# Four RMS norms whose scale is applied late: sums by one product with ones and roots over 512 columns, in place of eight narrow products and a spread

## The reference, cut to what matters

```python
def rms_norm(x, g):
    y = xf * lax.rsqrt(jnp.mean(xf * xf, axis=-1, keepdims=True) + EPS)
    return (y * g.astype(jnp.float32)).astype(x.dtype)

for i in range(DEPTH):                      # DEPTH = 2
    u = rms_norm(h, norm_mix_g[i])
    ...
    h = h + merged @ w_o[i]
    m = rms_norm(h, norm_mlp_g[i])
    h = h + jnp.square(jax.nn.relu(m @ w_up[i])) @ w_down[i]
    e = rms_norm(h, norm_ple_g[i])
    h = h + jax.nn.sigmoid(e @ w_ple_gate[i]) * (p[i] @ w_ple_proj[i])
```

## Time and profile before

| | us |
|---|---|
| median of 3 runs | 3181.43 (3177.78 to 3186.06) |
| the profiled execution, its own time | 3182.89 |
| its span | 3181.1 |
| TensorE busy | 3137.8 (99%), granted clock 0.993 on the mean |
| VectorE busy | 1957.7 (62%) |
| ScalarE busy | 1225.0 (39%) |
| GpSimd busy | 674.5 (21%) |
| mean DMA rate | 108 GB/s |

### The profile page before, as it was taken

How to read it: one execution, slowest core, us unless ns; L and a number is a source line. 1 busy time by engine, 2 the same in 40 slices (tenths; PEclk the granted TensorE clock), 3 DMA queues, 4 the chain that set the end, 5 groups by cost and what they waited for, 6 DMA issues and landing times.

```text
span 3181.1 us, 36265 instructions
## 1 busy us (share of the span) xinstructions
PE 3137.8 (99%) x14870; PEld 2547.1 (80%) x14870; DVE 1957.7 (62%) x2630; ACT 1225.0 (39%) x1645; POOL 674.5 (21%) x499
## 2 busy tenths in 40 slices
PE   9999999999999999999999999999999999999998
PEld 7877888888887788888888766778888888888887
DVE  7555657566666566677756556656555589963433
ACT  4234442233432344422244345643334353442222
POOL 1000000000100010699971133302433001110001
PEclk9999999999999999999999999999999999999999
DMA  3222233454222223355432100023333322222221
GB/s 132 77 95 84 87 139 141 164 197 180 91 88 90 80 86 111 132 202 186 172 113 100 31 25 28 18 84 129 118 124 115 144 86 101 103 95 95 95 104 67
DMA packets 55622, 342.41 MB, mean 108 GB/s; under 512 B 5984, under 2 KB 7840, under 8 KB 18208
## 3 DMA queue, kind: packets, MB, share of 16 engines
q1 hardware_dynamic: 54080, 337.46, 29.6%
q10 hardware_dynamic: 1376, 2.62, 0.2%
HBM read 327.47 MB, written 12.58 MB: 107 GB/s over the span
## 4 chain that ended last, share of the span: by engine, by line
PE 84%; DVE 9%; ACT 4%; issue 2%; POOL 1%; DMA 0%; DVEq 0%; ACTq 0%; SPq 0%; POOLq 0%
PE PS L264 83%; DVE wl L273 2%; DVE UL L273 1%; DVE FA L281 1%; ACT PB L270 1%; PE PS L267 1%; DVE SC L273 1%; ACT SC L270 1%; ACT UH L270 1%; DVE PB L273 1%; DVE SC L281 1%; POOL PB L277 1%; DVE ST L293 1%; DVE PS L273 0%; ACT wh L270 0%
## 5 line engine op out<-in xcount | busy, mean ns | idle before, releaser
L264 PE MATMUL PS<-UH,wh 128*128 128x512 f32 (+1 forms) x2120 | 836.3, 394 | 4.3 <-DVE UL L273 1.8
L264 PE MATMUL PS<-UH,wl 128*128 128x512 f32 (+1 forms) x2120 | 823.0, 388 | 0.0
L264 PE MATMUL PS<-UL,wh 128*128 128x512 f32 (+1 forms) x2120 | 822.9, 388 | 0.0
L273 DVE TENSOR_TENSOR wl<-raw,wh 128x2048 fp32r<-128x2048 f32 (+2 forms) x255 | 563.4, 2211 | 386.1 <-ACT wh L270 386.0
L264 PE MATMUL PS<-RH,wh 128*128 128x512 f32 (+2 forms) x1640 | 645.5, 394 | 2.1 <-ACT FA L270 1.1
L264 PE MATMUL PS<-RH,wl 128*128 128x512 f32 (+2 forms) x1640 | 639.0, 390 | 0.0
L264 PE MATMUL PS<-RL,wh 128*128 128x512 f32 (+2 forms) x1640 | 638.9, 390 | 0.0
L270 ACT ACTIVATE wh<-raw 128x2048 fp32r<-128x2048 f32 (+2 forms) x255 | 452.4, 1780 | 242.4 <-DMA raw<-in_wall 170.4
L264 PEld LDWEIGHTS PS<-UH,wh 128*128 128x128 f32 x2120 | 399.2, 188 | 109.3 <-issue 18.7
L264 PEld LDWEIGHTS PS<-UL,wh 128*128 128x128 f32 x2120 | 399.4, 188 | 82.9 <-issue 3.8
L264 PEld LDWEIGHTS PS<-UH,wl 128*128 128x128 f32 x2120 | 399.0, 188 | 82.8
(11 more groups left out here) (220 smaller groups left out, 3166.1 us busy)
## 6 DMA issues: line engine op xcount, KB each, us to landing
raw<-in_wall SPq DMA_DIRECT2D x224, 1024.0 KB, 4.9
FA<-in_wmod SPq DMA_DIRECT2D x48, 1024.0 KB, 4.9
raw<-in_wall SPq DMA_DIRECT2D x29, 512.0 KB, 3.5
kspec<-FA SPq DMA_DIRECT2D x8, 1024.0 KB, 6.4
FA<-kspec SPq DMA_DIRECT2D x8, 1024.0 KB, 6.9
PB<-in_window SPq DMA_DIRECT2D x16, 256.0 KB, 4.5
Hs<-in_xT ACTq DMA_DIRECT2D x4, 512.0 KB, 8.2
FA<-in_w SPq DMA_DIRECT2D x4, 512.0 KB, 5.7
```

The costliest lines, as they stand in the source:

```text
L264: return self.put(self.eng and self.eng.matmul(out, w, x, start=start, stop=stop, skip_group_check=True))
L273: return self.put(self.eng and self.eng.tensor_tensor(out, a, b, op))
```

## The change

In the four norms of `LATE`, GpSimd adds all eight squares into `SSQ`. TensorE then makes one product, ones (128x128, stationary) by `SSQ` (128x512), after 5 of the 8 steps of `first_x` (k == 4): it gives the sum of each column on all partitions. VectorE writes the mean plus EPS as 128x512 into `rstd(n)`, ScalarE takes the root there over 512 columns, VectorE the reciprocal over 512 columns. There are no diagonals, no `spread` and no last copy. In `rstd_all` the reciprocal stands behind `w_lo`, `pp_lo` and `pj_lo`. The other norms stay as they were.

```diff
@@ first_x
-                if n and k == 2:
+                if n and k == (4 if n in LATE else 2):
                     square_sums(n)
-                elif n and k == 5:
+                elif n and k == 5 and n not in LATE:
                     spread(n)
@@ square_sums
+            if n in LATE:
+                take(("ms", n), ("ms", n))
+                p.wait_ge("ssq", (n, 7))
+                p.matmul(ps(("ms", n)), ones, SSQ, True, True).then_inc("sum", ("ms", n))
+                return
@@ stream
-            freed = ("ssq", (n, k)) if k < 7 else ("sum", ("ms", n))
+            freed = ("ssq", (n, k)) if k < 7 or n in LATE else ("sum", ("ms", n))
@@ norm_root
-            a.activation(NST, NST, ACT.Sqrt).then_inc("rt", n)
+            a.activation(*((rstd(n), rstd(n)) if n in LATE else (NST, NST)), ACT.Sqrt).then_inc("rt", n)
@@ vector_program
+        def rstd_all(n):
+            v.wait_ge("sum", ("ms", n))
+            v.tensor_scalar(rstd(n), ps(("ms", n)), 1.0 / D, EPS, MUL, ADD).then_inc("ms", n)
+            if n in FIRST:
+                w_lo(FIRST[n], 2)
+            if n in (2, 5):
+                for k in range(2):
+                    h, lo = proj(512 * k, 512)
+                    v.wait_ge("pp_hi", (n // 3, k))
+                    v.tensor_tensor(lo, fa(512 * k, 512), h.bitcast(F32), SUB).then_inc("pp_lo", (n // 3, k))
+                projection_low(n // 3, 0)
+            v.wait_ge("rt", n)
+            v.reciprocal(rstd(n), rstd(n)).then_inc("rs", n)
+            v.settle()
+
         def rstd_h(n):
-
+            if n in LATE:
+                rstd_all(n)
+                return
@@ square_sum
-            for k in range(1, 7):
+            for k in range(1, 8 if n in LATE else 7):
```

## The result

| us | before | after |
|---|---|---|
| median of the runs of one comparison | 3183.59 (3177.78 to 3186.94, 12 runs) | 3192.68 (3186.34 to 3193.29, 12 runs) |
| the profiled execution, its own time | 3182.89 | 3192.91 |
| its span, mean granted clock | 3181.1, 0.993 | 3191.1, 0.989 |

The account below looks back on a forecast made before the run. The prediction took TensorE to bound the kernel, busy 3137.8 of 3181.1 us. Norms 1, 2, 4 and 5 gave +0.7, -1.1, +3.2 and +0.7, sum +3.5; on the median of 3181.4 that made 3185.0 us, range 3176 to 3191.

Parts of the forecast that it names:

- TensorE's saving of 1.81 us a norm: Each of four late norms: eight narrow products vanish, the new product costs the spread's 0.87 us; 7.2 us in all.
- the root's place: ScalarE, norm 1: the root starts at 464.03 instead of 461.85, 2.18 us later, and lasts 0.63 for 0.20.
- the first eviction's shift: VectorE, norm 1: the first eviction moves from 468.63 to 472.1, 3.5 us later, waiting for the root.
- the waits: TensorE waits for late lows: 2.5 us in norm 1, 0.7 in norm 2, 2.5 in norm 5.
- GpSimd's operations would not slow the reciprocal: Norm 4: by the page's port-lock rule, only the low waits beside GpSimd, not the reciprocal; the term is at most +3.9.
- the slower rival: Norm 4: reciprocal and `features` block each other, chain 10.0 us late; sum +10.3, 3191.7 us; chance 0.12.
- -1.8 + 2.5 = +0.7: Norm 1: TensorE's saving less its wait for the fourth weight piece's low, net +0.7 us.
- +3.5: Sum over the four late norms: 0.7 - 1.1 + 3.2 + 0.7 us.
- Behind it the chain catches up: Norm 1, after the 2.5 us wait for the fourth weight piece: the chain recovers; net stays +0.7 us.
- Norm 4's +3.2: Norm 4 has no slack, so TensorE loses the eviction chain's delay in full: +3.2 us, between +1.9 and +6.6.
- The floor from GpSimd: Behind norm 4, at the gate's first weight piece: GpSimd 4.9 us late makes TensorE at least 1.9 late.
- 3182 to 3189: Whole kernel: the main forecast's range with the bounds of norm 4, all within 0.3%; forecast chance 0.62.

Follow-up runs that it names:

- experiments 2: Changed kernel with 11, 17 and 11 idle matmuls, results unread, where TensorE waits in norms 1, 4 and 5: 3185.48 us, ratio 1.0004.
- 10: Changed kernel with 11 idle matmuls in the waits of norms 1 and 5 each, none in norm 4's: 3186.00 us, ratio 1.0004.
- Experiment 5: Changed kernel with the product with ones at k == 2 and the reciprocal ahead of the third piece's low in norms 1 and 4: 3180.93 us, ratio 0.9990.
- 1: Changed kernel with the product with ones after 3 of the 8 steps of first_x (k == 2), not after 5: 3182.14 us, ratio 0.9991.
- 3: Kernel before with GpSimd adding all eight squares in the late norms and four narrow products for eight, narrow root and spread kept: 3183.44 us, ratio 0.9996.
- experiment 9: Changed kernel again, unaltered, for a second comparison and profile against the kernel before: 3190.28 us, ratio 1.0020.

## Why the prediction was wrong

**What held.** TensorE's saving of 1.81 us a norm, the root's place, the reciprocal of 3.35 us, the first eviction's shift, and the waits: 2.40, 0.69 and 2.49 us where 2.5, 0.7 and 2.5 stood. Also that GpSimd's operations would not slow the reciprocal, beside them 3.34 us: the slower rival's mechanism did not occur, though its 3191.7 us is near the measured time. That was the right size for another reason.

**The step that failed** is the sum of each norm, "-1.8 + 2.5 = +0.7" and its like: it counts a wait of TensorE at its own length. The first row after each long wait shows that it costs more, since the matmuls behind it run at half the clock, for 7 to 11 of them. That term stood at nothing, with no reason given; it was 5.5 us in this profile, and experiments 2 and 10 take it away, norm by norm, by filling the waits. With it, and 2.5 us less for the sizes below, +3.5 becomes the +6.5 that the four norms show; the two comparisons gave +9.1 and +5.7 us by their medians. "Behind it the chain catches up" was true of the chain and silent on the clock.

**Sizes off.** Norm 4's +3.2: the chain's shift was +2.15 at the first eviction and +1.8 at the fourth piece's low, since the third piece's low took 3.00 us beside GpSimd and not the 4.61 of before. In experiments 2, 5, 1 and 3 it took 3.01, 2.60, 4.05 and 4.60 us; what decides it wasn't tried. The floor from GpSimd didn't bind: the first wait was already longer. Experiment 5 shows it at work once that wait is short, at the product and at the projection's low in place of the gate's first piece. Two small waits of the kernel before behind norm 4 (0.39 and 0.65 us over a step) vanished; I hadn't counted them. The forecast's own range, "3182 to 3189", doesn't follow from the bounds of norm 4, which give 3183.7 to 3188.4; neither reaches the measured time.

**What stays open.** The remaining 3.5 us between the first two profiles comes from falls of the clock outside the four norms, which differ from execution to execution (experiment 9), and of which the medians share an unknown part; why the first comparison had no execution near 3183 us, where the second had three of eleven, isn't settled. Nor is why a wait of one length is followed by the lower clock in one execution and not in the next.

## What to carry to other kernels

Where TensorE is the bound, a new wait in its stream isn't priced at its length: in these norms one of up to 1.63 us cost just that, and ten of the eleven from 2.30 us on cost 1.5 to 3 us more. Between them nothing was tried in these norms, and elsewhere in the same kernel even a wait of 1.80 us was followed by the lower clock in all twelve profiles. So a change that takes work off TensorE and delays what it waits for should first be laid out so that the delay stays small (issue the product earlier, put the long operation where its engine is idle), and the same change then turned from +0.28% to -0.23%. After each repair look for the next wait, because an earlier TensorE meets the next late engine.

## What was not expected of the hardware

Seven profiles hold eleven unfilled waits for lows of 2.30 to 3.91 us in these norms. Ten were followed by the lower clock (the exception is one of 2.40 us); none of those up to 1.63 us was. The fall came at once or up to 1.3 us after the restart and lasted 7 to 14 matmuls; in the two profiles of the changed kernel the wait of 3.91 us cost 2.25 and 2.67 us of clock, that of 2.40 us 1.73 and nothing. It is no rule for the whole kernel: of four waits in the stages that the change doesn't touch, that of 1.80 us was followed by the lower clock in twelve of twelve profiles, those of 2.1, 2.3 and 2.8 us in nine each. And it takes no wait: in ten of the twelve profiles the clock falls near 904 as well, in the kernel before behind 34 products of two columns (3.5 us), with TensorE's rows without a gap. Matmuls whose results nobody reads kept the clock up through 2.4 to 3.9 us of waiting, and were worth 5 to 7 us to the kernel by the medians, 4.1 in the trace of these norms.
